# In attention, the copy and the sum of a unit's two result halves stand one group further forward in two engines' orders

## The reference, cut to what matters

```python
s_win = einsum(q_r, k_win) * scale + bias          # 8 rows x 16 columns around the query
s_ctx = einsum(q_r, k_ctx) * scale                 # 256 context tokens
p = softmax(concatenate([s_win, s_ctx]))
o = einsum(p_win, v_win) + einsum(p_ctx, v_ctx)    # then o @ w_o
```

## Time and profile before

| what | value |
| --- | --- |
| median of 3 runs | 3192.97 us (3192.13 to 3195.08) |
| profiled execution, its own time | 3193.72 us |
| span of its profile | 3191.9 us |
| mean granted clock of TensorE | 0.973 of full speed |
| TensorE matmuls busy | 2973.9 us, 93% of the span |
| VectorE / ScalarE / GpSimd busy | 1829.6 / 814.6 / 739.1 us |
| first and last sum of the halves (L1631), 64 in all | 1814.7 and 2316.9 us |

### The profile page before, as it was taken

One profiled execution on the slowest core, in us unless ns is written; L12 is line 12 of the kernel. 1 busy time (PEld: TensorE's weight loads), 2 busy tenths in 40 slices (PEclk: granted clock), 3 DMA queues, 4 the chain that ended last, 5 costly groups with the idle time before them and its releaser, 6 DMA issues.

```text
span 3191.9 us, 44786 instructions
## 1 busy us (share of the span) xinstructions
PE 2973.9 (93%) x15690; PEld 2475.2 (78%) x15690; DVE 1829.6 (57%) x3065; ACT 814.6 (26%) x1425; POOL 739.1 (23%) x457
## 2 busy tenths in 40 slices
PE   4999999799999999999969899999797999999996
PEld 1788887478888888888759788888675888888884
DVE  2676665667666677654551366666615555555556
ACT  2311111321111111111142366666623111111112
POOL 0211111021111111111111354545421222222210
PEclk8999999899999999999989999999899999999998
DMA  6121213022122221211035556554630111111111
GB/s 257 64 66 53 85 62 89 0 70 78 55 74 73 74 79 54 74 40 40 33 103 124 164 150 175 164 154 140 182 137 26 39 56 42 42 57 39 59 39 59
DMA packets 178763, 269.29 MB, mean 84 GB/s; under 512 B 70656, under 2 KB 122880, under 8 KB 178688
## 3 DMA queue, kind: packets, MB, share of 16 engines
q1 hardware_dynamic: 178688, 268.32, 27.2%
HBM read 222.13 MB, written 50.07 MB: 85 GB/s over the span
## 4 chain that ended last, share of the span: by engine, by line
PE 77%; DVE 8%; issue 5%; ACT 4%; DMA 3%; SPq 1%; POOL 1%; DVEq 0%; POOLq 0%; ACTq 0%
PE psum L705 41%; PE psum L736 19%; PE psum L878 4%; PE psum L857 3%; PE psum L932 2%; PE psum L901 2%; PE psum L915 2%; DVE residual L1396 1%; DMA o_dram<-o_st_lo 1%; DVE prod L1376 1%; PE psum L773 1%; PE psum L671 1%; DVE more_acc L1452 1%; PE psum L722 1%; ACT squares L1032 1%
## 5 line engine op out<-in xcount | busy, mean ns | idle before, releaser
L1396 DVE SCALAR_TENSOR_TENSOR residual<-psum,modulation,residual 128x512 f32<-128x512 f32 (+1 forms) x1072 | 717.6, 689 | 831.5 <-PE psum L736 828.2
L1737 POOL TENSOR_TENSOR w_lo<-raw,w_hi 128x1024 fp32r<-128x1024 f32 x196 | 493.2, 2529 | 1919.5 <-ACT w_hi L1026 1916.7
L705 PE MATMUL psum<-act_hi,w_hi 128*128 128x512 f32 (+1 forms) x2208 | 589.9, 367 | 9.5 <-POOL w_lo L1737 7.6
L705 PE MATMUL psum<-act_lo,w_hi 128*128 128x512 f32 (+1 forms) x2208 | 589.5, 367 | 0.0
L705 PE MATMUL psum<-act_hi,w_lo 128*128 128x512 f32 (+1 forms) x2208 | 588.6, 367 | 0.0
L705 PEld LDWEIGHTS psum<-act_hi,w_hi 128*128 128x128 f32 x2208 | 397.9, 188 | 88.5 <-issue 6.3
L1026 ACT ACTIVATE w_hi<-raw 128x1024 fp32r<-128x1024 f32 x196 | 203.8, 1060 | 1000.5 <-PE psum L705 939.4
L736 PE MATMUL psum<-prod_hi,w_hi 128*128 128x512 f32 (+1 forms) x1072 | 409.2, 382 | 33.0 <-DVE residual L1396 15.1
L705 PEld LDWEIGHTS psum<-act_lo,w_hi 128*128 128x128 f32 x2208 | 380.4, 188 | 70.8
L705 PEld LDWEIGHTS psum<-act_hi,w_lo 128*128 128x128 f32 x2208 | 380.4, 188 | 70.4
L736 PE MATMUL psum<-prod_hi,w_lo 128*128 128x512 f32 (+1 forms) x1072 | 395.9, 369 | 0.0
(11 more groups left out here) (124 smaller groups left out, 3782.7 us busy)
## 6 DMA issues: line engine op xcount, KB each, us to landing
raw<-ffn_panels SPq DMA_DIRECT2D x132, 512.0 KB, 5.0
mod_in<-mod_rest SPq DMA_DIRECT2D x64, 384.0 KB, 3.2
raw<-conv_panels SPq DMA_DIRECT2D x32, 512.0 KB, 5.3
mod_raw<-mod_panels SPq DMA_DIRECT2D x24, 512.0 KB, 11.2
more_row<-mod_panels SPq DMA_DIRECT2D x48, 256.0 KB, 2.8
k_hi<-k_dram SPq DMA_DIRECT2D x32, 320.0 KB, 5.7
k_lo<-k_dram SPq DMA_DIRECT2D x32, 320.0 KB, 7.3
v_st<-v_dram SPq DMA_DIRECT2D x32, 320.0 KB, 7.2
```

Of the source, the lines that this page charges most:

```text
L705: mm = pe.matmul(psum[:, bank + b, 0:tn], w[:, s, kb, :], acts[h][:, kb, t0:t0 + tn], start=(kb == 0 and n == 0), stop=(kb == KB - 1 and n ...
L1396: dve.scalar_tensor_tensor(out=residual[:, ob, t0:t0 + tn], in0=psum[:, 6 + r % 2, 0:tn], scalar=modulation[:, gates + ob, kind_of(t0):kin ...
L1737: pool.tensor_tensor(panel(w_lo, s), raw[:, s], panel(w_hi, s), ALU.subtract).then_inc(lo_done[s], 1)
```

## The change

On ScalarE, `half` of the unit before moves from behind group 1 (and its drain) to directly behind `pt_high` of group 0, ahead of the drain of group 0. On VectorE, `head_sum` of the unit before moves from behind group 1 and both `invert` to directly behind `pt_low` of group 0, ahead of the drain and of `invert(.., 0)`. No operation is added or removed, and the orders of TensorE, GpSimd and SP stay.

```diff
@@ ScalarE, attention
                     pt_high(i, u, 0)
+                    if not (first and u == 0):
+                        half(*before(i, u))
                     drain(group0[u])
                     if more:
                         exponentials(nxt_i, nxt_u, 1)
                     pt_high(i, u, 1)
                     drain(group0[u] + 1)
-                    if not (first and u == 0):
-                        half(*before(i, u))
                     pt_high(i, u, 2)
@@ VectorE, attention
                     pt_low(i, u, 0)
+                    if not (first and u == 0):
+                        head_sum(*before(i, u))
                     drain(group0[u])
                     if not (last and u == UNITS - 1):
                         invert(nxt_i, nxt_u, 0)
...
                     drain(group0[u] + 1)
                     if not (last and u == UNITS - 1):
                         invert(nxt_i, nxt_u, 1)
-                    if not (first and u == 0):
-                        head_sum(*before(i, u))
                     if not (last and far_u < 2):
                         bias_scores(far_i, far_u, 0)
                     pt_low(i, u, 2)
```

## The result

The changed kernel takes 3216.89 us (median of 6 runs, 3212.0 to 3220.39) against 3192.55 us for the one before in the same series: 1.0079 times as long, 95% interval 1.0067 to 1.0091. The forecast named the direction, but its 3208.4 us and its range (up to 3213.0) lie too low. The profiled execution took 3219.86 us, with a span of 3218.1 us: 26.2 us more than before. It is the figure the steps are held against.

The account below looks back on a forecast made before the run. TensorE was taken to set the pace. Pairs 0 to 5 (+6.7 us), pair 6 (+1.3), its DMA stall (+1.5) and pair 7 (+5.9) sum to +15.4, against the median 3208.4 us; range 3199.0 to 3213.0.

Parts of the forecast that it names:

- The copy stands still until E: ScalarE's moved copy waits for the end of the previous unit's last value matmul (E), delaying everything behind it.
- the waits go and nothing takes their place: Rival: TensorE's 12.8 us of waits for the sum vanish and blocked steps arrive in time; 3180.2 us, chance 0.04.
- Units 1, 2, 3 and 5: Steady pairs: unit 1 costs +0.51 us (late drain), unit 3 +0.80 (drain behind copy), units 2 and 5 nothing.
- Unit 4: Steady pairs: projection about in time, GpSimd's normalise some 0.1 us too late; net +0.15 us.
- Unit 6: Steady pairs: drain of group 21 behind the copy delays the projection, part of the sum's wait given back; net +0.2 us.
- The stall in pair 6: ScalarE's 11.4 us store wait behind backlogged DMAs: unit 3's store about 1.5 us later, all of it counted, +1.5.
- Units 7 and 0 together: Steady pairs: unit 7's delay of 0.66 us hidden, unit 0's gain bounded by GpSimd; net -0.34 to -0.7, taken -0.55.
- Pair 7: Last pair, without projections: VectorE's chain of bias steps starts later behind the moved copy; +5.9 us, bounds 2.5 and 6.5.
- the last rival: New waits stay and TensorE's clock drops in pair 7: at most +8.4 us more, 3216.8 us, chance 0.04.
- The clock in steady pairs: New TensorE gaps in steady pairs are about 1 us, so the granted clock stays; nothing added.

Follow-up runs that it names:

- exp_first: Changed kernel, but the copy stands behind the second exponential, just ahead of group 1's copy, the sum ahead of group 1's low part; 3194.17 us, 1.0011 of the kernel before.
- low_first: Changed kernel, but in unit 4 GpSimd makes the low part of unit 3's sum ahead of its second normalise; 3213.71 us, 1.0071 of the kernel before.
- v_first: Kernel before, but SP loads the next pair's values ahead of its queries and keys; copy and sum at their old places; 3205.68 us, ratio 1.0046.
- unit0_only: Kernel before, with copy and sum moved forward in unit 0 of each pair alone; 3187.68 us, 0.9992 of the kernel before.
- units_0_3: Kernel before, with unit 0 in the changed order and unit 3 of pairs 0 to 6 as in exp_first; 3184.84 us, ratio 0.9984.
- last_pair_old: Changed kernel in pairs 0 to 6, with the old order in pair 7; 3210.41 us, 1.0063 of the kernel before.
- drain_first: Changed kernel, but group 0's drain goes ahead of the moved copy on ScalarE and the moved sum on VectorE; 3208.88 us, 1.0056 of the kernel before.
- heads_first: Changed kernel, but SP loads the next pair's first head (q, k) ahead of the store of unit 3; 3241.14 us, 1.016 of the kernel before.

## Why the prediction was right in direction and too small in size

**The copy stands still until E, and what is behind it waits.** Right: 60 of 64 copies wait for TensorE, 83.9 us in all, and exp_first takes the loss of units 1, 3, 4 and 7 away by this alone. The rival "the waits go and nothing takes their place" had its first half: the 12.8 us are gone; between 1800 us and the last value matmul the gaps of TensorE's matmuls add up to 64.0 us, where they were 38.0.

**Units 1, 2, 3 and 5.** Right in place and size: 0.53 for 0.51, 0.93 for 0.80, 0 for 0 twice. The 0.13 of unit 3 is mostly the gap between the copy and the next step on ScalarE (above). Unit 4 took 0.31 for 0.15.

**Unit 6: the step that failed.** I priced the drain of group 21 alone ("Unit 6 ... Net +0.2"). low_first, without the late store, gives 0.35, so this part was nearly right, but the term was 1.26 in the mean of pairs 1 to 5 and 6.6 over pairs 0 to 5, where I had 1.2: 5.4 of the missing 12 us. The drop of the clock in pair 1 makes 1.6 of these 5.4, and the waits for the keys the rest. I had seen in pair 6 that the store of unit 3 comes some 1.5 us later and that the next loads stand behind it ("The stall in pair 6"), and didn't ask the same for pairs 0 to 5, though that chain is the same in each. It measured 1.85. The trace before gave the slack to compare it with: in pair 3 the last load of the keys was issued at 2044.4 and landed 7.4 us later, and TensorE used them at 2051.91, 0.1 us behind that. A wait of up to 0.76 us would have cost nothing, as five pairs of the changed kernel and pair 4 of v_first show; the waits of 1.1 to 2.0 us were longer.

**Units 7 and 0 together.** I took -0.55; they came to +0.17. Unit 7 costs 0.84 for the 0.66 forecast. GpSimd's `normalise` behind the tables bounds unit 0's gain as I said (TensorE waits for POOL's `probs` there, 0.17 to 0.63 us in pairs 1, 4 and 5), but I held the start of the tables for fixed. It hangs on ScalarE's `out_high` of unit 6, which waits for a store behind the late loads: where this wait was 1.26 us (pair 0), unit 0 of the next pair gained 0.35, and where it was 0.02 (pair 1), 1.12. With the store of unit 3 earlier (low_first), unit 0 gains 1.06 and the two together are -0.23. Up to the end of pair 5 (six units 7, five units 0) I had -2.1 and it was +1.7: 3.8 us. Its DMA part is shown; the remaining 0.3 a pair is the size of unit 7 and the bound of GpSimd.

**The stall in pair 6 and pair 7's start.** I had 1.1 for this stretch, it was 0.4. Units 0 to 3 of pair 6 came to +0.4 (forecast 0.1); from unit 4 on I had the 1.5 of the stall less 0.5 for unit 0 of pair 7, and it was 0.0. Inside it, unit 4 cost 1.9, unit 6 2.2 and unit 7 0.2, unit 5 gave 1.0 back and unit 0 of pair 7 3.4; the longest wait of ScalarE for the store is 9.9 us and was 11.4. So the backlog's end did not move fully with its start, and some 0.5 of the +1.5 came, if unit 0 of pair 7 gained its 0.5. This is one pair of traces, and the same stretch moves by -0.9 in unit0_only and by -2.1 in units_0_3, where of it only unit 0 of pair 7 was moved. So how much the stall absorbs stays open.

**Pair 7.** Forecast 6.4 behind unit 0, measured 8.1, and its own by last_pair_old. Units 1, 2 and 3 cost 1.64, 1.48 and 1.64 (forecast 1.5 each), unit 4 0.13 (0.2), unit 5 -0.34 (-0.4), unit 7 0.32 (0.5). Unit 6 cost 3.27, not 1.6, and this is the last rival in one place: behind a gap of 1.94 us the granted clock fell. The window of the changed kernel that starts 0.16 us behind this gap, and the same of drain_first, where the unit cost 1.76 with a gap of 1.94 as well:

```profile
2335.00:2340.00 5.00, 4.75 (x28) 4.57 (x28) 1.56 (x3) 1.43 (x3) 1.64 (x2) 0.66 0.26 54
```

```profile
2324.59:2329.59 5.00, 4.05 (x32) 3.49 (x31) 2.80 (x6) 2.90 (x6) 1.63 (x2) 1.00 0.23 48
```

A group of four turns took 1.09 us there in place of 0.66. The runs low_first (clock 0.66, cost 3.19) and heads_first (1.00, 1.76) divide in the same way. So of the rival's +8.4 us about 1.5 came, in one unit of eight. The clock rule that the prediction cites from the Trainium skill ("TensorE: Matmul & The Clock Gate", "What's actually happening") agrees with the trace in this: each of the five stretches at the 1.2 GHz level in the attention of the changed kernel begins in or behind a gap of 1.9 us or more.

**The clock in steady pairs.** The prediction put the clock at nothing there, since its gaps were of about 1 us. It had left out the keys' waits of up to 2 us, and in pair 1 the clock fell behind one of them (above): 1.6 us. The length of a gap doesn't tell whether the clock falls behind it: one of 1.93 us brought it down and one of 2.02 did not, and in drain_first a wait of 2.43 us left it at 1.00 (unit 6 of pair 1: 9.73 us busy, as in the pairs without a drop).

Sum of what was missing: 5.4 (unit 6), 3.8 (units 7 and 0), 1.0 (unit 4), 0.8 (unit 3), 0.1 (unit 1), less 0.1 (units 2 and 5), less 0.7 (pair 6 and the stall), and 1.7 (pair 7) make 12.0; with the 15.4 of the forecast 27.4, as measured. Of the 12.0, 3.1 are the clock's (unit 6 of pairs 1 and 7). Why the keys' wait itself differs between 1.07 and 2.02 us from pair to pair stays open.

## What to carry to other kernels

Moving an instruction forward in an in-order engine moves its wait forward too: ask first whether its operand is ready at the new place. If it is not, the engine's whole standing time belongs to everything behind it. Then follow the delay through every queue to its end, the DMA queue's included: here the largest part of what I had missed came some 18 us behind the copy that stood still (2046.5 to 2064.3 in pair 3), by a store behind which loads stood that had next to no slack. And a new gap on TensorE can cost more than its length, when the clock falls behind it. A move pays where the operand is already there: that was one unit of eight at the new place, and unit 3 half a step further on. Where it is not, the order of what stands behind decides: in exp_first the copy of unit 4 waited 0.4 us and the unit still gained 0.67.

## What the runs showed of the hardware that was not expected

TensorE's granted clock fell in the midst of steady pairs that keep it busy for 92% of the time and more, behind single waits of 1.8 to 2.4 us: once in the changed kernel and five times in v_first. The same 64 matmuls then took 11.3 us and not 9.75, so that a wait of 1.93 us cost 2.74 and one of 2.02 us cost 1.26. Other waits of up to 2.43 us left the clock at 1.00.

A 64x256 copy on ScalarE (0.38 us) held the next instruction's start for 0.41 us from its own start when that was the drain's copy (all 13 times in the changed kernel; 2038.06 to 2038.46 is one), and for 0.28 when it was an exponential (2046.54 to 2046.82). Behind an exponential the next start comes 0.1 before the recorded end.

A store of 64 KB issued behind six loads (heads_first, the store of unit 3) landed 6.3 to 6.9 us behind its issue. In the changed kernel the median from issue to landing of such stores was 2.0 us in the steady pairs, the longest 8.0.
